# Expert weights in slabs of 1 MB in eighteen places instead of 2 MB in nine

## The chip, the cores and the metric

The kernel runs on one core of a Trainium2 chip. The metric is the time of one launch on the device in microseconds (us); lower is better. All arithmetic is float32. The engines are named as the profile names them: PE (TensorE, the matmuls; PEld its weight loads), DVE (VectorE), ACT (ScalarE), POOL (GpSimd) and SP (SyncE, which here only issues DMAs).

## The reference

One step of a two-layer backbone for 128 context tokens and 256 latent tokens of width 1024. Each layer has three token mixers, a merge, and then a mixture of 16 experts. The change touches only how the weights of the experts reach the core:

```python
def _expert_choice_ffn(h, w_router, w_gate, w_up, w_down):
    cap = EC_FACTOR * n // N_EXPERTS
    aff = jax.nn.softmax(jnp.einsum('bnd,de->bne', h, w_router), axis=-1)
    g, idx = lax.top_k(jnp.swapaxes(aff, 1, 2), cap)
    xg = jax.vmap(lambda hb, ib: hb[ib])(h, idx)
    hid = jax.nn.silu(jnp.einsum('becd,edf->becf', xg, w_gate)) * jnp.einsum('becd,edf->becf', xg, w_up)
    out = jnp.einsum('becf,efd->becd', hid, w_down) * g[..., None]
    ... # added back to the tokens it was taken from
```

Each of `w_gate`, `w_up` and `w_down` is 1024 x 1024 float32 per expert, 4 MB. So 16 experts with three matrices are 192 MB per layer (201.3 million bytes), and nothing of them is used twice.

## The kernel before

The loop over the two layers is a loop on the chip (`nc.Fori`); its body is one block in which each engine has its own program. The programs meet at semaphores: `gate_h`, `up_h`, `down_full` count the slabs of each kind that PE has used, and `expert_in[b]` says that a load into buffer b has landed. In time a layer has a dense part (modulation, the three mixers, projections), the routing (affinities, the choice of tokens), and the expert stage.

The expert stage: an expert's matrix is cut along its rows into two slabs of four row chunks (128 partitions x 4 x 1024, 2 MB, `EXPERT_SLABS = 6` per expert). The slabs go round nine places in SBUF (`EXPERT_BUFFERS = 9`): four are the ring of the dense part, three lie in `dense`, two in `wide`. `EXPERT_ORDER` fixes the order both for SP and for PE: gate and up of expert e + 1 come before down of expert e. SP issues one DMA per slab (`load_expert`); before load i it waits until PE has used slab i - 9 (`wait_used`). PE (`product`) waits at each slab for its landing, runs eight pairs of matmuls (a pair fills two halves of the array, 64 columns each) and then counts the slab as used.

The first three loads are issued between dense slabs 27, 28 and 29, as soon as their places are free (`EARLY`, `buffer_free`); the other six follow as the ring and the two last places come free, all before the expert stage begins. At the end of a layer SP loads the first four modulation slabs of the next layer into the ring (`mod_again`), each after the last expert slab in its place has been used. The one in ring place 0 waits for slab 95, the very last. When all engines are through, `clear_all` sets all the semaphores of the layer to zero, each engine a fifth of them, between two barriers, and the loop jumps back.

The weights are laid out in HBM by `expert_slabs` so that each slab is one contiguous piece, with 16 KB in a row for each partition. The dense part's slabs are fetched in two DMAs of 1 MB each (lines 580 and 581), with 8 KB in a row for each partition.

Of the kernel before, what the change touches and what calls it, by code (L numbers as in the profile page):

```python
# [13 lines left out]
P = 128  # L14
D = 1024
KD = D // P
# [24 lines left out]
DENSE_SLABS = 32  # L41
EXPERT_SLABS = 6
EXPERT_BUFFERS = 9
MOD_AHEAD = 4
# [69 lines left out]
def build(nc, x_in, cvec, cache_kT, cache_v, state_in_dram, w_mod, layer_vectors, layer_scalars,  # L114
# [13 lines left out]
    with ctx:  # L128
# [83 lines left out]
        def ring_slab(r):  # L212
            return slab_shape(ring[:, r].rearrange("p k n -> p (k n)"))
# [5 lines left out]
        wide_1 = slab_shape(wide_cols[:, 4096:8192])  # L219
        BUFFERS = [dense_1, dense_2, wide_1, ring_slab(1), dense_0, ring_slab(0), ring_slab(2), ring_slab(3), wide_0]  # L220
        RING_AT = [5, 3, 6, 7]
# [238 lines left out]
        with nc.Fori(0, DEPTH) as layer:  # L460
            with nc.Block() as block:
# [23 lines left out]
                def mod_parts(j):  # L485
# [9 lines left out]

                EXPERT_ORDER = ([(0, s) for s in range(4)]
                                + [x for e in range(NE) for x in [(e + 1, s) for s in range(4) if e + 1 < NE] + [(e, 4), (e, 5)]])
                assert len(EXPERT_ORDER) == NE * EXPERT_SLABS
# [44 lines left out]
                def _(sp):  # L543
# [4 lines left out]
                    def load_expert(i):  # L548
                        e, s = EXPERT_ORDER[i]
                        w = (w_gate, w_up, w_down)[s // 2]  # L550
                        sp.dma_start(BUFFERS[i % EXPERT_BUFFERS], w[layer, e, s % 2]).then_inc(expert_in[i % EXPERT_BUFFERS], 16)

                    def wait_used(i):
                        e, s = EXPERT_ORDER[i]
                        sp.wait_ge((gate_h, up_h, down_full)[s // 2], 2 * e + s % 2 + 1)

                    EARLY = 3

                    def buffer_free(i):

                        if i < EARLY:
                            sp.wait_ge(c_done, HEADS_C)
                            sp.wait_ge(ko_st, 32)
                            sp.wait_ge(v_stored, 32)
                        elif i == 4:
                            sp.wait_ge(br_full, 3 * KD)
                        elif i == 8:
                            sp.wait_ge(w_full, KD)
                            sp.wait_ge(stored, 32)
                        else:  # L570
                            wait_slab_free(sp, DENSE_SLABS - RING + RING_AT.index(i))

                    for n in range(MOD_AHEAD, DENSE_SLABS):
                        if 27 <= n < 27 + EARLY:
                            buffer_free(n - 27)
                            load_expert(n - 27)
                        wait_slab_free(sp, n - RING)
# [12 lines left out]
                    def mod_again(j):  # L590
                        i = max(i for i in range(NE * EXPERT_SLABS) if i % EXPERT_BUFFERS == RING_AT[j])
                        wait_used(i)
                        mod_ahead(sp, DEPTH - 1 - layer, j)
# [33 lines left out]
                def _(pe):  # L627
# [330 lines left out]
                    def product(expert, s0, bank, signal, lhsT):  # L958

                        for s in (s0, s0 + 1):  # L960
                            i = EXPERT_ORDER.index((expert, s))
                            w = BUFFERS[i % EXPERT_BUFFERS]
                            pe.wait_ge(expert_in[i % EXPERT_BUFFERS], 16 * (i // EXPERT_BUFFERS + 1))
                            for kk in range(KD // 2):
                                k = (s % 2) * (KD // 2) + kk
                                for half in range(2):
                                    last = M.matmul(psum[HALF * half:HALF * (half + 1), bank, :], lhsT(k),  # L967
                                                    w[:, kk, half * SLAB:(half + 1) * SLAB], start=k == 0, stop=k == KD - 1)
                            last.then_inc(signal, 1)
# [15 lines left out]
                    def up_product(expert):  # L985
                        if expert >= 1:
                            pe.wait_ge(hid_ready, expert)
                        product(expert, 2, S[1], up_h, gathered_chunk(expert))

# [8 lines left out]
                    def down_product(expert):  # L998
                        pe.wait_ge(ht_read, expert + 1)
                        if expert >= 1:  # L1000
                            pe.wait_ge(down_act, expert)
                            pe.wait_ge(down_dve, expert)
                        product(expert, 4, TR[1], down_full, lambda k: hidT[:, k % 4, k // 4, :])

# [43 lines left out]
                def _(sc):  # L1048
# [208 lines left out]
                    def silu(expert):  # L1257
                        sc.wait_ge(gate_h, 2 * expert + 2)
                        if expert >= 1:
# [5 lines left out]
                    for e in range(NE):  # L1265
# [5 lines left out]
                        if nth == 2 and quad + 1 < QUADS:  # L1271
                            read_gathered(quad + 1)
                        sc.wait_ge(down_full, 2 * e + 2)
                        for half in range(2):
# [6 lines left out]
                def _(dve):  # L1281
# [269 lines left out]
                    def gated(expert):  # L1551
                        dve.wait_ge(silu_ready, expert + 1)
                        dve.wait_ge(up_h, 2 * expert + 2)
                        if expert >= 1:
# [14 lines left out]
                    for e in range(NE):  # L1569
# [10 lines left out]
                        if nth == 2 and quad + 1 < QUADS:  # L1580
                            read_gathered(quad + 1)
                        dve.wait_ge(down_full, 2 * e + 2)
                        for half in range(2):
# [115 lines left out]
```

## Time and profile before

| | |
|---|---|
| time, median of 3 runs | 2063.16 us (2059.74 to 2064.07) |
| time of the profiled execution | 2063.99 us |
| its span, first to last instruction | 2062.1 us |
| mean granted TensorE clock | 0.984 |
| PE busy | 1857.9 us, 90% of the span |
| read from HBM | 555.30 MB, 271 GB/s over the span |
| expert products of layer 1 on PE | 579.1 to 1018.0 us |
| expert products of layer 2 on PE | to 2034.9 us |

The span is 1.9 us shorter than the execution. The page cuts the span into 40 slices of 51.6 us; a digit is a busy share in tenths. A matmul's float32 operands make two instructions of it, so eight pairs of matmuls are 32 instructions in two slabs and 16 in one. MB in the profile are millions of bytes where it speaks of traffic, and KB are 1024 bytes where it speaks of one DMA: a slab of 2048 KB is 2.097 million bytes.

### The profile page before, as it was taken

To read this page: it belongs to the slowest core of one execution; us is meant where nothing else is said; L and a number is where in the kernel's file an instruction comes from. 1 tells how busy PE (TensorE), PEld (TensorE's weight loads), DVE (VectorE), ACT (ScalarE), POOL (GpSimd) and SP (SyncE) were. 2 spreads that over 40 slices of the span, in tenths; PEclk is the share of its full clock that TensorE was granted. 3 is DMA by queue.
4 is the path that set the end of the run, shared out by engine and by line. 5 is a ranking of instruction groups with operands and counts; after the bars stand their busy time and mean duration, and the time that the engine had idled before them with its cause. 6 is when DMAs were issued, how large, how long until landed. Compare 5 with 4: busy or idle time off the path is not lost. (4 is left out here: it accounts for less than half of the span.)

```text
span 2062.1 us, 20148 instructions
## 1 busy us (share of the span) xinstructions
PE 1857.9 (90%) x8062; PEld 929.3 (45%) x8062; DVE 614.7 (30%) x1179; ACT 336.0 (16%) x771; POOL 36.7 (2%) x22
## 2 busy tenths in 40 slices
PE   5999999999799988788689999999997998888885
PEld 2565556555444333233245555565554343333322
DVE  2332346554311101001142324654534002010103
ACT  4022331000201000000131223210002010100001
POOL 0100000000000000000020000000000000000000
PEclk9999999999999999999989999999998999999998
DMA  9322281433469999999972222816332999999998
GB/s 391 139 92 87 82 349 70 168 158 129 157 284 427 428 427 428 428 427 427 402 307 92 82 87 87 332 41 244 119 142 107 400 427 428 427 427 428 428 427 345
DMA packets 53412, 560.88 MB, mean 272 GB/s; under 512 B 6080, under 2 KB 10816, under 8 KB 12224
## 3 DMA queue, kind: packets, MB, share of 16 engines
q1 hardware_dynamic: 49536, 556.90, 65.2%
q10 hardware_dynamic: 3776, 2.62, 0.4%
q8 instruction: 66, 1.08, 0.2%
q14 instruction: 34, 0.28, 0.0%
HBM read 555.30 MB, written 4.19 MB: 271 GB/s over the span
## 5 line engine op out<-in xcount | busy, mean ns | idle before, releaser
L685 PE MATMUL psum<-hT,ring 128*128 128x384 f32 x768 | 259.5, 493 | 4.1 <-DMA ring<-in_w_in 2.2
L812 PE MATMUL psum<-hT,ring 128*128 128x384 f32 x768 | 255.9, 486 | 1.1 <-issue 1.1
L967 PE MATMUL psum<-dense 128*64 128x512 f32 x864 | 195.4, 596 | 33.4 <-DMA dense<-in_w_up 17.6
L967 PE MATMUL psum<-ring,dense 128*64 128x512 f32 x832 | 188.3, 596 | 25.4 <-DMA ring<-in_w_gate 14.6
L812 PEld LDWEIGHTS psum<-hT,ring 128*128 128x128 f32 x768 | 145.6, 190 | 102.5 <-issue 1.5
L685 PEld LDWEIGHTS psum<-hT,ring 128*128 128x128 f32 x768 | 145.0, 192 | 99.2 <-issue 6.7
L1556 DVE TENSOR_TENSOR state<-state,psum 128x512 f32<-128x512 f32 x32 | 22.0, 688 | 375.3 <-PE psum L967 337.2
L967 PEld LDWEIGHTS psum<-dense 128*64 128x64 f32 x864 | 63.9, 137 | 155.0 <-issue 130.7
L967 PE MATMUL psum<-ring,bwd_decay 128*64 128x512 f32 x512 | 115.3, 596 | 20.1 <-DMA ring<-in_w_down 20.1
L896 PE MATMUL psum<-dense,ring 128*128 128x384 f32 x384 | 131.9, 487 | 0.0
L687 PE MATMUL psum<-ring,hT 128*128 128x512 f32 x288 | 126.5, 592 | 0.0
L1452 DVE RECIPROCAL kcT<-kcT 128x384 f32<-128x384 f32 x48 | 122.6, 2553 | 1.7
L967 PEld LDWEIGHTS psum<-ring,dense 128*64 128x64 f32 x832 | 60.7, 137 | 138.3 <-issue 117.9
L1275 ACT ACTIVATE kcT<-psum 32x512 f32<-32x512 f32 x64 | 37.6, 588 | 480.5 <-PE psum L967 480.1
L896 PEld LDWEIGHTS psum<-dense,ring 128*128 128x128 f32 x384 | 72.8, 190 | 50.6
L1584 DVE COPY q_decay<-psum 16x512 f32<-16x512 f32 x32 | 21.9, 684 | 239.4 <-PE psum L967 239.4
L967 PE MATMUL psum<-wide,dense 128*64 128x512 f32 x352 | 80.1, 597 | 14.0 <-DMA wide<-in_w_gate 13.8
L908 PE MATMUL psum<-wide,ring 128*128 128x384 f32 x256 | 82.9, 486 | 0.0
L687 PEld LDWEIGHTS psum<-ring,hT 128*128 128x128 f32 x288 | 54.3, 190 | 62.2 <-issue 60.3
L967 PE MATMUL psum<-wide,bwd_decay 128*64 128x512 f32 x320 | 72.7, 595 | 10.7 <-DMA wide<-in_w_down 10.7
L660 PE MATMUL psum<-ring,silu_c 128*32 128x512 f32 x384 | 50.1, 649 | 35.5 <-DMA ring<-in_w_mod 21.0
L967 PEld LDWEIGHTS psum<-ring,bwd_decay 128*64 128x64 f32 x512 | 35.8, 137 | 96.9 <-issue 68.6
(201 smaller groups left out, 1579.5 us busy)
## 6 DMA issues: line engine op xcount, KB each, us to landing
ring<-in_w_up SPq DMA_DIRECT2D x32, 2048.0 KB, 38.4
ring<-in_w_down SPq DMA_DIRECT2D x32, 2048.0 KB, 40.2
ring<-in_w_in SPq DMA_DIRECT2D x60, 1024.0 KB, 9.1
dense<-in_w_up SPq DMA_DIRECT2D x30, 2048.0 KB, 40.2
dense<-in_w_gate SPq DMA_DIRECT2D x24, 2048.0 KB, 35.6
ring<-in_w_gate SPq DMA_DIRECT2D x20, 2048.0 KB, 36.8
wide<-in_w_down SPq DMA_DIRECT2D x20, 2048.0 KB, 40.3
wide<-in_w_gate SPq DMA_DIRECT2D x20, 2048.0 KB, 38.3
```

What stands on the lines that cost most here:

```text
L660: last = M.matmul(psum[32 * q:32 * q + 32, bank, :], silu_c[:, k, :], ring[:, n % RING, k, :], start=half == 0, stop=half == 1)
L685: last = M.matmul(psum[:, bank, 0:T], ring[:, n % RING, k, cols], hT[:, k, :], start=k == 0, stop=k == KD - 1)
L687: last = M.matmul(psum[:, bank, :], hT[:, k, cols], ring[:, n % RING, k, :], start=k == 0, stop=k == KD - 1)
L812: last = M.matmul(psum[:, Z[1], 0:T], ring[:, n_gate % RING, k, (j % 4) * P:(j % 4 + 1) * P], hT[:, k, :], start=k == 0, stop=k == KD - 1)
L896: last = M.matmul(psum[:, Z[0], 0:T], w[:, k, j * P:(j + 1) * P], zT[:, source + k, :], start=k == 0, stop=k == 3)
L908: last = M.matmul(psum[:, S[j % 2], 0:T], ring[:, (30 + j // 4) % RING, k, (j % 4) * P:(j % 4 + 1) * P], merged[:, k, :], start=k == 0, st ...
L967: last = M.matmul(psum[HALF * half:HALF * (half + 1), bank, :], lhsT(k), w[:, kk, half * SLAB:(half + 1) * SLAB], start=k == 0, stop=k == ...
L1275: last = A_.activation(out_lat[half][SLOTS * nth:SLOTS * (nth + 1)], psum[HALF * half:HALF * half + CAP_LAT, TR[1], :], ACT.Copy)
L1452: then(V.reciprocal(g, g))
L1556: V.tensor_tensor(hid, act, psum[:, S[1], :], ALU.mult).then_inc(hid_ready, 1)
L1584: last = V.tensor_copy(out_ctx[half][SLOTS * nth:SLOTS * nth + CAP_CTX], psum[HALF * half + CAP_LAT:HALF * half + ROWS, TR[1], :])
```

## The change

A matrix is cut into four slabs of two row chunks (1 MB), each of the nine places is halved into two buffers, and every count goes over from 2 to `PER_PRODUCT = 4` slabs per matrix. The layout in HBM changes with it: a slab is again one contiguous piece, now with 8 KB in a row for each partition. The places, the order of the matrices, the matmuls and the bytes are the same; the first three places are still filled early, now with two loads each. Nine semaphores are added.

```diff
@@ -39,8 +39,9 @@
 SLAB = 512
 RING = 4
 DENSE_SLABS = 32
-EXPERT_SLABS = 6
-EXPERT_BUFFERS = 9
+EXPERT_SLABS = 12
+PER_PRODUCT = 4
+EXPERT_BUFFERS = 18
 MOD_AHEAD = 4
 
 DVE_MODULATES = ((0, 2, 3, 5, 6), (2, 4, 7))
@@ -217,7 +218,8 @@
         dense_2 = slab_shape(dense[:, DENSE - 4096:DENSE])
         wide_0 = slab_shape(wide_cols[:, 0:4096])
         wide_1 = slab_shape(wide_cols[:, 4096:8192])
-        BUFFERS = [dense_1, dense_2, wide_1, ring_slab(1), dense_0, ring_slab(0), ring_slab(2), ring_slab(3), wide_0]
+        PLACES = [dense_1, dense_2, wide_1, ring_slab(1), dense_0, ring_slab(0), ring_slab(2), ring_slab(3), wide_0]
+        BUFFERS = [place[:, 2 * half:2 * half + 2, :] for place in PLACES for half in range(2)]
         RING_AT = [5, 3, 6, 7]
         assert len(BUFFERS) == EXPERT_BUFFERS
 
@@ -493,8 +495,8 @@
                             + [(6, j, "T") for j in range(4)] + [(7, j, "rows") for j in range(NBLK)]
                             + [(8, j, "T") for j in range(4)])
 
-                EXPERT_ORDER = ([(0, s) for s in range(4)]
-                                + [x for e in range(NE) for x in [(e + 1, s) for s in range(4) if e + 1 < NE] + [(e, 4), (e, 5)]])
+                EXPERT_ORDER = ([(0, s) for s in range(8)]
+                                + [x for e in range(NE) for x in [(e + 1, s) for s in range(8) if e + 1 < NE] + [(e, s) for s in range(8, 12)]])
                 assert len(EXPERT_ORDER) == NE * EXPERT_SLABS
                 UNITS = 12
                 A_STEPS = UNITS + 2
@@ -547,18 +549,19 @@
                     sp.dma_start(kcT[:], cache_kT[layer]).then_inc(keys_in, 16)
                     def load_expert(i):
                         e, s = EXPERT_ORDER[i]
-                        w = (w_gate, w_up, w_down)[s // 2]
-                        sp.dma_start(BUFFERS[i % EXPERT_BUFFERS], w[layer, e, s % 2]).then_inc(expert_in[i % EXPERT_BUFFERS], 16)
+                        w = (w_gate, w_up, w_down)[s // PER_PRODUCT]
+                        sp.dma_start(BUFFERS[i % EXPERT_BUFFERS], w[layer, e, s % PER_PRODUCT]).then_inc(expert_in[i % EXPERT_BUFFERS], 16)
 
                     def wait_used(i):
                         e, s = EXPERT_ORDER[i]
-                        sp.wait_ge((gate_h, up_h, down_full)[s // 2], 2 * e + s % 2 + 1)
-
-                    EARLY = 3
+                        sp.wait_ge((gate_h, up_h, down_full)[s // PER_PRODUCT], PER_PRODUCT * e + s % PER_PRODUCT + 1)
+
+                    EARLY = 6
 
                     def buffer_free(i):
 
-                        if i < EARLY:
+                        i = i // 2
+                        if i < 3:
                             sp.wait_ge(c_done, HEADS_C)
                             sp.wait_ge(ko_st, 32)
                             sp.wait_ge(v_stored, 32)
@@ -571,9 +574,10 @@
                             wait_slab_free(sp, DENSE_SLABS - RING + RING_AT.index(i))
 
                     for n in range(MOD_AHEAD, DENSE_SLABS):
-                        if 27 <= n < 27 + EARLY:
-                            buffer_free(n - 27)
-                            load_expert(n - 27)
+                        if 27 <= n < 30:
+                            for i in (2 * (n - 27), 2 * (n - 27) + 1):
+                                buffer_free(i)
+                                load_expert(i)
                         wait_slab_free(sp, n - RING)
                         to, of = slab_into(n), slab_source(n)
                         half = to.shape[1] // 2
@@ -588,7 +592,7 @@
                                 sp.dma_start(bias[b], rpb_bias[layer, b]).then_inc(bias_in, 16)
 
                     def mod_again(j):
-                        i = max(i for i in range(NE * EXPERT_SLABS) if i % EXPERT_BUFFERS == RING_AT[j])
+                        i = max(i for i in range(NE * EXPERT_SLABS) if i % EXPERT_BUFFERS == 2 * RING_AT[j] + 1)
                         wait_used(i)
                         mod_ahead(sp, DEPTH - 1 - layer, j)
 
@@ -957,12 +961,12 @@
 
                     def product(expert, s0, bank, signal, lhsT):
 
-                        for s in (s0, s0 + 1):
+                        for s in range(s0, s0 + PER_PRODUCT):
                             i = EXPERT_ORDER.index((expert, s))
                             w = BUFFERS[i % EXPERT_BUFFERS]
                             pe.wait_ge(expert_in[i % EXPERT_BUFFERS], 16 * (i // EXPERT_BUFFERS + 1))
-                            for kk in range(KD // 2):
-                                k = (s % 2) * (KD // 2) + kk
+                            for kk in range(2):
+                                k = (s % PER_PRODUCT) * 2 + kk
                                 for half in range(2):
                                     last = M.matmul(psum[HALF * half:HALF * (half + 1), bank, :], lhsT(k),
                                                     w[:, kk, half * SLAB:(half + 1) * SLAB], start=k == 0, stop=k == KD - 1)
@@ -985,7 +989,7 @@
                     def up_product(expert):
                         if expert >= 1:
                             pe.wait_ge(hid_ready, expert)
-                        product(expert, 2, S[1], up_h, gathered_chunk(expert))
+                        product(expert, PER_PRODUCT, S[1], up_h, gathered_chunk(expert))
 
                     def hidden_transposed(expert):
                         pe.wait_ge(hid_ready, expert + 1)
@@ -1000,7 +1004,7 @@
                         if expert >= 1:
                             pe.wait_ge(down_act, expert)
                             pe.wait_ge(down_dve, expert)
-                        product(expert, 4, TR[1], down_full, lambda k: hidT[:, k % 4, k // 4, :])
+                        product(expert, 2 * PER_PRODUCT, TR[1], down_full, lambda k: hidT[:, k % 4, k // 4, :])
 
                     def picks_transposed(quad):
                         pe.wait_ge(pick_g_ready, quad + 1)
@@ -1255,7 +1259,7 @@
                                           psum[:, XG[part], :].rearrange("p (k s) -> p k s", s=CAP_LAT), ACT.Copy).then_inc(xg_act, 1)
 
                     def silu(expert):
-                        sc.wait_ge(gate_h, 2 * expert + 2)
+                        sc.wait_ge(gate_h, PER_PRODUCT * (expert + 1))
                         if expert >= 1:
                             sc.wait_ge(hid_ready, expert)
                         A_.activation(act, psum[:, S[0], :], ACT.Silu).then_inc(silu_ready, 1)
@@ -1270,7 +1274,7 @@
                         A_.activation(hidT.rearrange("p q h s -> p (q h s)"), psum[:, TR[0], :], ACT.Copy).then_inc(ht_read, 1)
                         if nth == 2 and quad + 1 < QUADS:
                             read_gathered(quad + 1)
-                        sc.wait_ge(down_full, 2 * e + 2)
+                        sc.wait_ge(down_full, PER_PRODUCT * (e + 1))
                         for half in range(2):
                             last = A_.activation(out_lat[half][SLOTS * nth:SLOTS * (nth + 1)], psum[HALF * half:HALF * half + CAP_LAT, TR[1], :], ACT.Copy)
                         last.then_inc(down_act, 1)
@@ -1550,7 +1554,7 @@
 
                     def gated(expert):
                         dve.wait_ge(silu_ready, expert + 1)
-                        dve.wait_ge(up_h, 2 * expert + 2)
+                        dve.wait_ge(up_h, PER_PRODUCT * (expert + 1))
                         if expert >= 1:
                             dve.wait_ge(ht_full, expert)
                         V.tensor_tensor(hid, act, psum[:, S[1], :], ALU.mult).then_inc(hid_ready, 1)
@@ -1579,7 +1583,7 @@
                             gated(e + 1)
                         if nth == 2 and quad + 1 < QUADS:
                             read_gathered(quad + 1)
-                        dve.wait_ge(down_full, 2 * e + 2)
+                        dve.wait_ge(down_full, PER_PRODUCT * (e + 1))
                         for half in range(2):
                             last = V.tensor_copy(out_ctx[half][SLOTS * nth:SLOTS * nth + CAP_CTX], psum[HALF * half + CAP_LAT:HALF * half + ROWS, TR[1], :])
                         last.then_inc(down_dve, 1)
@@ -1658,7 +1662,7 @@
         return w.reshape(d, rows // P, P, n, cols // n).transpose(0, 3, 2, 1, 4)
 
     def expert_slabs(w):
-        return w.reshape(DEPTH, NE, 2, KD // 2, P, D).transpose(0, 1, 2, 4, 3, 5)
+        return w.reshape(DEPTH, NE, 4, 2, P, D).transpose(0, 1, 2, 4, 3, 5)
 
     feeds = [
         ("x", x.reshape(T, KD, P).transpose(2, 1, 0)),
```

On SP, around the start of the expert stage: before, with the last loads into fresh places and the first refills. The names `gate_h` and `up_h` are the counts of gate and up slabs used by PE.

```order
L551 DMA ring<-in_w_up 128x4096 [waits w_full] x2
L551 DMA wide<-in_w_down 128x4096 [waits stored,w_full]
L551 DMA dense<-in_w_down 128x4096 [waits gate_h]
L551 ISA [waits gate_h]
L551 DMA dense<-in_w_gate 128x4096
```

The same place after the change:

```order
L553 DMA ring<-in_w_up 128x2048 [waits w_full] x4
L553 DMA wide<-in_w_down 128x2048 [waits stored,w_full] x2
L553 DMA dense<-in_w_down 128x2048 [waits gate_h] x2
L553 ISA [waits gate_h]
L553 DMA dense<-in_w_gate 128x2048
L553 ISA [waits gate_h]
L553 DMA dense<-in_w_gate 128x2048
```

Each load has become two of half the width, with a wait of its own before each; nothing has changed places.

On PE, the last products of a layer (down of expert 15) and what follows them, before:

```order
L967 MATMUL psum<-dense,bwd_decay 64x512 [waits down_dve,expert_in4,down_act,ht_read]
L967 MATMUL psum<-dense,bwd_decay 64x512 x7
L967 MATMUL psum<-ring,bwd_decay 64x512 [waits expert_in5]
L967 MATMUL psum<-ring,bwd_decay 64x512 x7
L1024 MATMUL psum<-square,q_decay 128x128 [waits pgT_read,down_dve,down_act]
```

And after:

```order
L971 MATMUL psum<-dense,bwd_decay 64x512 [waits down_dve,expert_in8,down_act,ht_read]
L971 MATMUL psum<-dense,bwd_decay 64x512 x3
L971 MATMUL psum<-dense,bwd_decay 64x512 [waits expert_in9]
L971 MATMUL psum<-dense,bwd_decay 64x512 x3
L971 MATMUL psum<-ring,bwd_decay 64x512 [waits expert_in10]
L971 MATMUL psum<-ring,bwd_decay 64x512 x3
L971 MATMUL psum<-ring,bwd_decay 64x512 [waits expert_in11]
L971 MATMUL psum<-ring,bwd_decay 64x512 x3
L1028 MATMUL psum<-square,q_decay 128x128 [waits pgT_read,down_dve,down_act]
```

Behind the wait for the last load there stand 4 matmuls of this listing where there were 8.

The semaphores cleared by PE at the end of a layer, before and after:

```order
L397 ISA x26
```

```order
L399 ISA x27
```

PE has one more; SP has 28 instead of 26, and the other three engines have 27 instead of 25.

## Rows read from the trace of the kernel before

**Rows 1.** The page, slices of 51.6 us: DMA share in tenths and rate.
```profile
DMA  9322281433469999999972222816332999999998
GB/s 391 139 92 87 82 349 70 168 158 129 157 284 427 428 427 428 428 427 427 402 307 92 82 87 87 332 41 244 119 142 107 400 427 428 427 427 428 428 427 345
```
**Rows 2.** Windows: length, busy of each engine, PEclk, DMA share, GB/s.
```profile
560.00:580.00 20.00, 11.40 (x82) 10.37 (x82) 9.42 (x34) 5.76 (x10) 0.00 (x0) 0.83 0.00 1
600.00:1000.00 400.00, 349.61 (x1690) 136.27 (x1691) 52.97 (x104) 37.62 (x64) 0.00 (x0) 1.00 1.01 428
1620.00:2010.00 390.00, 342.12 (x1658) 133.90 (x1654) 52.28 (x103) 36.47 (x62) 0.00 (x0) 1.00 1.01 428
```
**Rows 3.** The page's DMA issues: count, KB each, median us to landing.
```profile
ring<-in_w_up SPq DMA_DIRECT2D x32, 2048.0 KB, 38.4
ring<-in_w_down SPq DMA_DIRECT2D x32, 2048.0 KB, 40.2
```
**Rows 4.** Timeline of PE: stage start, then end of layer 1.
```profile
579.10 7.09 PE L967 MATMUL psum<-dense 128*64 128x512 f32 x32 [0.83 <-issue]
585.99 3.63 PE L967 MATMUL psum<-wide,dense 128*64 128x512 f32 x16
...
999.77 3.65 PE L967 MATMUL psum<-wide,bwd_decay 128*64 128x512 f32 x16 [1.33 <-DMA wide<-in_w_down]
1004.59 3.65 PE L967 MATMUL psum<-ring,bwd_decay 128*64 128x512 f32 x16 [1.16 <-DMA ring<-in_w_down]
1008.17 0.66 PE L429 MATMUL psum<-const,state 128*128 128x128 f32 x4
1010.15 3.65 PE L967 MATMUL psum<-dense,bwd_decay 128*64 128x512 f32 x16 [1.32 <-ACT bwd_decay L1270]
1014.37 3.65 PE L967 MATMUL psum<-ring,bwd_decay 128*64 128x512 f32 x16 [0.57 <-DMA ring<-in_w_down]
1019.57 0.46 PE L1024 MATMUL psum<-square,q_decay 128*128 128x128 f32 x2 [1.55 <-ACT kcT L1275]
```
**Rows 5.** Timeline of SP's DMA issues: stage start, then end of layer 1.
```profile
547.56 0.33 SPq L551 DMA_DIRECT2D wide<-in_w_down  x1
582.78 0.33 SPq L551 DMA_DIRECT2D dense<-in_w_down  x1
586.35 0.33 SPq L551 DMA_DIRECT2D dense<-in_w_gate  x1
...
1008.53 11.07 SPq L416 DMA_DIRECT2D ring<-in_w_mod  x4
```
**Rows 6.** Windows of 20 us in which loads of 8 KB rows fill the queue.
```profile
275.00:295.00 20.00, 16.59 (x148) 8.08 (x150) 7.78 (x21) 7.08 (x22) 0.00 (x0) 1.00 1.01 424
1293.00:1313.00 20.00, 17.09 (x156) 7.97 (x157) 7.72 (x21) 7.18 (x21) 0.00 (x0) 1.00 1.01 424
272.00:292.00 20.00, 17.41 (x156) 8.58 (x158) 8.81 (x25) 7.17 (x22) 0.00 (x0) 1.00 1.00 418
1290.00:1310.00 20.00, 17.40 (x158) 8.40 (x150) 7.79 (x21) 6.99 (x21) 0.00 (x0) 1.00 1.01 419
```
**Rows 7.** Timeline of PE: the first matmul of layer 2.
```profile
1036.21 4.50 PE L660 MATMUL psum<-ring,silu_c 128*32 128x512 f32 x20 [11.16 <-issue]
```
**Rows 8.** PE's semaphore clears by their line: ns min/median/max.
```profile
L397 PEldq EVENT_SEMAPHORE_RANGE_CLEAR  x53: 56/56/63, 10.5 to 2046.1; - x53
```
**Rows 9.** Timeline of SP: the slowest issues of loads in layer 2.
```profile
1049.62 1.01 SPq L580 DMA_DIRECT2D ring<-in_w_in  x1
1050.81 1.97 SPq L581 DMA_DIRECT2D ring<-in_w_in  x1
```

## The prediction

> **What bounds the kernel now.** I read the slices first. In both layers there is a stretch of eight slices, the expert stage, in which the DMA digit is 9 and the rate stands at 427 or 428 GB/s [rows 1]. Over 400 us of it in layer 1 and 390 us in layer 2 the mean is 428 GB/s and the 16 DMA engines are fully busy, while PE is busy for 349.61 of 400 us [rows 2]. So the transfers set the pace there. The second look is at the landing times: a 2 MB load lands 38.4 to 40.2 us after its issue [rows 3]. One slab takes 2,097,152 bytes / 428 GB/s = 4.90 us, so about eight loads are queued all the time. PE takes a slab as it lands (1.15 to 1.33 us of waiting before slabs that it then works through in some 3.4 us [rows 4]) and gives its place back at once.
>
> The third look is at both ends of this stream. Before the stage all nine places are full and the DMA engines stand still: the last load into a fresh place is issued at 547.56, and the rate is 1 GB/s from 560 to 580 [rows 2, 5]. PE starts the first product at 579.10; 32 instructions, two slabs, take until 585.99, so one slab takes 3.44 us [rows 4]. The first refill is issued at 582.78 [rows 5], which is 579.10 + 3.44 + 0.24. From there 96 - 9 = 87 slabs have to come: 87 x 4.90 = 426.3 us, and with 5.3 us for the start and the landing that makes the 431.6 us until the last one is there at 1014.37 [rows 4]. PE then needs 3.65 us for the whole last slab before the results can be read and scattered. Layer 2 has the same shape. So three things of this stage are on the path to the end: when the first place comes free, the rate, and how much work is left once the last bytes are in.
>
> **The change part by part.**
>
> The start. The first place comes free after half a slab, 3.44 / 2 = 1.72 us earlier. The first refill has only 1 MB, 2.45 us of transfer, but the next is issued 1.72 us later, so the stream doesn't stop, just as now 3.57 us lie between issues and 4.90 us are needed [rows 5]. The whole stream moves forward: -1.72 us in each layer. The bounds are 0, if the start of the stream costs more with small loads, and the whole 1.72.
>
> The end. After the last landing there stand 4 pairs of matmuls instead of 8: 3.65 / 2 = 1.83 us, of which I take 1.72 by the pace of the start. What else could be late then? The slab before it started at 1010.15, held up by the transposed hidden values and not by its data: these came after down of expert 14, whose last slab landed at 1004.59 [rows 4]. That step also shrinks by half a slab, so it is ready by about 1008.4, and PE has 1014.37 - 1008.4 = 6.0 us for the three quarter-matrices before the last, 5.2 us of work. It is just through when the last 1 MB lands. Then -1.72 us in each layer; the bound on the other side is 0 if the last megabyte has to queue behind something.
>
> The two ends together: 4 x 1.72 = 6.9 us to gain.
>
> The rate. The trace has no 1 MB expert load, but the dense part loads its slabs in halves of 1 MB with 8 KB rows, and twice several of them stand in the queue together. In the stretches 275 to 295 and 1293 to 1313 the DMA engines are as busy as in the expert stage and move 424 GB/s. Windows that begin 3 us earlier show 418 and 419 [rows 6]; the queue is just filling up in these, so I take 424. Then the stream of a layer takes 426.3 x (428/424 - 1) = 4.0 us longer, 8.0 us in both. Bounds: 0 (nothing is lost by the smaller rows: the windows are short, and 1% of 20 us is 0.2 us, less than one packet of each engine), and 426.3 x (428/418 - 1) = 10.2 us in each layer. The nearest rows are the full windows, so the value is 4.0.
>
> The Trainium skill, "DMA: Bandwidth & Descriptors", section "Measured (HBM→SBUF, 128 partitions, SWDGE, issued from GpSimd)", warns against small transfers: a fixed 2.0 us per DMA beside the bytes at 436 GB/s. If each queued load paid that, a layer's 87 slabs of 2 MB would take 87 x 6.8 = 592 us by an estimate from that page, and 174 halves 766; the trace disagrees, with 431.6 us, because eight loads are queued and the fixed part lies beside them. Its section "Why small descriptors are slow (HBM only)" gives about 3 cycles per packet on top of one per 32 bytes. As an estimate from that, two rows of 8 KB cost 2 x 259 cycles against 515, 0.58% more, 2.5 us per layer in place of 4.0; the sum below would then be -1.7 us instead of +1.3. The direction agrees with 424 against 428, and the size can't be told from windows of 20 us.
>
> SP. It issues 174 refills per layer instead of 87. An issue takes 0.33 us [rows 5], against 2.45 us of transfer, so it keeps up, and what stands behind it in its queue is only the next load. With twice as many loads outstanding the issue itself may stall, as it does when many dense loads are queued (1.01 and 1.97 us [rows 9]); that is still under 2.45 us, and the queue is full when it happens. Cost 0. PE has a wait per 4 pairs instead of 8; where the data are there, two slabs follow each other without a gap [rows 4], so 0 as well.
>
> The end of the layer. The next layer's first matmul comes 11.16 us after the last of this one [rows 7]; in that gap the semaphores are cleared. One more clear on PE is 0.056 us [rows 8], with what lies around it I take 0.1, per layer; bounds 0 and the whole gap divided by 26, 0.43. Sum 0.2 us. The modulation slabs of the next layer are issued as before after the last expert slab (four issues from 1008.53 on [rows 5]); they shift forward with it. Instructions of PE's program and the matmuls stay as they are.
>
> The sum: -6.9 + 8.0 + 0.2 = +1.3 us on the profiled execution's 2063.99, so 2065.3. The median of the runs shown is 2063.16, 0.8 us below the profiled one; measured against it the forecast is 2064.5 us.
>
> **The rivals.** About 0.2% (4.1 us) is what a measurement of this kernel can tell from no change.
>
> Rival 1, the rate isn't touched. For it: the engines are over 100% busy in both kinds of stretches, packets overlap, and the sample of 8 KB rows is 40 us long. Against it: two separate windows show the same 424. It gives -6.9 + 0.2 = -6.7 us, 2057.3 on the profiled execution and 2056.5 against the median: faster. It counts as faster as soon as the rate is at least 427.
>
> Rival 2, the stream of small loads is slower than the best windows. Mechanism: the DMA queue in the expert stage with 1 MB loads, each with its own completion, and PE, which has no slack against it. The mean of the four windows in rows 6 is 421 GB/s. Then the two streams cost 2 x 426.3 x (428/421 - 1) = 14.2 us, and the sum is -6.9 + 14.2 + 0.2 = +7.5 us, 2071.5 or 2070.7 against the median: slower. It decides where the loss is above 6.9 + 4.1 - 0.2 = 10.8 us, which is a rate under 422.6. For it: the windows of 418 and 419. Against: these begin while the queue fills.
>
> Rival 3, SP's issue becomes the bound. If every issue of a 1 MB load took longer than 2.45 us, the stream would be issue-bound; at 2.6 us it would cost 174 x 0.15 = 26 us in each layer. The longest single issue of these loads seen is 1.97 us [rows 9]. Unlikely.
>
> Rival 4, the small slabs don't bring the stream forward, because the rate in its first microseconds or the landing of the last load is set by something else. Then the gain is half or less: -3.4 + 8.0 + 0.2 = +4.8 us, 2068.8. For it: 5.3 us of the 431.6 aren't explained by bytes. Against: the refill is issued when a count of PE moves, and that is plain in rows 4 and 5.
>
> **How the numbers follow.** Forecast 0.50, rival 1 0.26, rival 2 0.16, rival 3 0.02, rival 4 0.06. Faster than before by over 0.2%: 0.26. Within: 0.50. Slower: 0.16 + 0.02 + 0.06 = 0.24. The forecast's own range is 2060.5 to 2067.4, from rates of 426 to 422.6. For 8 in 10 the range takes in rivals 1 and 2: 2056 to 2071.
>
> **What would show it.** In the changed profile: the first refill issued about 1.7 us nearer to the first product than the 3.68 us of now; the last landing followed by about 1.8 us of products; a window over the stage with 424 GB/s; about sixteen loads queued, so again some 40 us to landing; and the stage from its first product to its last longer by 4.0 - 3.4 = 0.6 us than now. A rate of 427 or more would make the forecast wrong on the fast side, one of 421 on the slow side. A DMA share under 1 in the stage would point to SP.

## The result

| | before | after |
|---|---|---|
| median of 11 runs each | 2063.16 us | 2072.93 us |
| ratio, 95% interval | 1 | 1.0038 (1.0029 to 1.0046) |
| profiled execution | 2063.99 us | 2071.03 us |
| span | 2062.1 us | 2068.9 us |

The change makes the kernel slower: 0.38%, 7.8 us (6.0 to 9.5). The two medians alone lie further apart, 9.8 us; the means of the 11 runs are 2064.0 and 2072.0 us. The profiled executions differ by 7.0 us, the spans by 6.8.

The windows of the kernel after come first (length, busy of each engine, PEclk, DMA share, GB/s), against [rows 2] and [rows 6]: the expert stages of both layers, then the four stretches of the dense part.

```profile
600.00:1000.00 400.00, 357.77 (x1684) 129.05 (x1686) 52.27 (x103) 37.61 (x64) 0.00 (x0) 1.00 1.01 421
1620.00:2010.00 390.00, 349.29 (x1648) 126.56 (x1648) 52.29 (x103) 36.46 (x62) 0.00 (x0) 1.00 1.01 421
...
275.00:295.00 20.00, 16.63 (x149) 8.14 (x151) 7.78 (x21) 7.23 (x22) 0.00 (x0) 1.00 1.01 424
1293.00:1313.00 20.00, 17.41 (x156) 8.19 (x149) 7.98 (x22) 6.82 (x22) 0.00 (x0) 1.00 1.01 419
272.00:292.00 20.00, 17.42 (x160) 8.61 (x160) 8.89 (x25) 7.32 (x23) 0.00 (x0) 1.00 1.00 417
1290.00:1310.00 20.00, 17.12 (x152) 8.91 (x152) 9.44 (x28) 8.15 (x26) 0.00 (x0) 1.00 0.99 408
```

The DMA engines are as full as before, and the rate of the expert stage is 421 GB/s instead of 428. The dense part was not changed. Its windows of layer 1 read 424 and 417, and 424 and 418 before [rows 6]. Those of layer 2 read 419 and 408 instead of 424 and 419, but by then this kernel is 3.25 us later in its work (the first matmul of layer 2 starts at 1039.46 instead of 1036.21 [rows 7]). Moved by these 3.25 us, the two windows read 424 and 419, as before:

```profile
1296.25:1316.25 20.00, 17.18 (x158) 7.99 (x157) 7.70 (x21) 7.28 (x21) 0.00 (x0) 1.00 1.01 424
1293.25:1313.25 20.00, 17.41 (x158) 8.39 (x150) 7.78 (x21) 7.00 (x21) 0.00 (x0) 1.00 1.01 419
```

So the 424 of the dense part comes back in another execution, and it still isn't the rate of the expert stage with 1 MB loads. Nor is a single window of 20 us exact: the 20 windows of that length between 600 and 1000 us read 424 to 429 GB/s before and 419 to 422 after.

The timeline of SP after, the last fill and the first refills:

```profile
548.15 1.07 SPq L553 DMA_DIRECT2D wide<-in_w_down  x2
581.09 2.05 SPq L553 DMA_DIRECT2D dense<-in_w_down  x2
584.65 2.05 SPq L553 DMA_DIRECT2D dense<-in_w_gate  x2
```

PE's timeline after, from the first product, and the end of layer 1:

```profile
579.12 7.09 PE L971 MATMUL psum<-dense 128*64 128x512 f32 x32 [0.83 <-issue]
...
1009.13 1.94 PE L971 MATMUL psum<-ring,bwd_decay 128*64 128x512 f32 x8 [0.56 <-DMA ring<-in_w_down]
1011.00 0.66 PE L431 MATMUL psum<-const,state 128*128 128x128 f32 x4
1012.98 3.65 PE L971 MATMUL psum<-dense,bwd_decay 128*64 128x512 f32 x16 [1.32 <-ACT bwd_decay L1274]
1016.58 1.94 PE L971 MATMUL psum<-ring,bwd_decay 128*64 128x512 f32 x8
1019.06 1.94 PE L971 MATMUL psum<-ring,bwd_decay 128*64 128x512 f32 x8 [0.54 <-DMA ring<-in_w_down]
1022.54 0.46 PE L1028 MATMUL psum<-square,q_decay 128*128 128x128 f32 x2 [1.55 <-ACT kcT L1279]
...
1039.46 6.55 PE L664 MATMUL psum<-ring,silu_c 128*32 128x512 f32 x32 [11.44 <-issue]
```

The first refill goes out 581.09 - 579.12 = 1.97 us after the first product instead of 3.68 [rows 4, 5]. The scatter begins 1022.54 - 1019.06 = 3.48 us after the last landing instead of 5.20 [rows 4]. Both ends gave the 1.7 us that was expected of them. But the last landing is 1019.06 - 579.12 = 439.94 us after the first product, where it was 435.27. From the first product to the scatter (the matmuls that add the experts' results back to the tokens), which I call the stage, it is 443.42 us, and was 1019.57 - 579.10 = 440.47. That is +2.95 us in layer 1. In layer 2 it is 2042.90 - 1599.27 = 443.63 against 440.41, +3.22 us. The gap with the semaphore clears is 0.28 us longer [rows 7].

The page's DMA issues after, answering to [rows 3]:

```profile
ring<-in_w_up SPq DMA_DIRECT2D x64, 1024.0 KB, 26.9
ring<-in_w_down SPq DMA_DIRECT2D x64, 1024.0 KB, 26.8
```

And SP's issues by the load's line, durations in ns, min/median/max:

```profile
L553 SPq DMA_DIRECT2D ring<-in_w_up x64: 332/2070/7792, 503.3 to 1957.7; - x64
```

A load lands after 26.9 us, not after some 40, and an issue takes 2.07 us instead of 0.33: SP stands at the issue. At 2.49 us per load 10.8 loads are on their way, not sixteen. That the issue waits for room in the queue is a reading; the run with a short queue below bears it out.

### The profile page after: what moved, and what is told of

Read it like the earlier page. It is cut to its first block and busy times, and to the rows that moved or that the text cites. A ratio compares the mean times of both kernels' runs of the same rounds, so it can differ in the third digit from the quotient of the medians.

```text
span 2068.9 us, 20622 instructions
## 1 busy us (share of the span) xinstructions
PE 1877.9 (91%) x8062; PEld 914.7 (44%) x8062; DVE 613.4 (30%) x1179; ACT 335.7 (16%) x771; POOL 36.4 (2%) x22
## 5 line engine op out<-in xcount | busy, mean ns | idle before, releaser
L971 PE MATMUL psum<-dense 128*64 128x512 f32 x864 | 201.5, 599 | 28.3 <-DMA dense<-in_w_up 15.4
L971 PE MATMUL psum<-ring,dense 128*64 128x512 f32 x832 | 194.0, 599 | 21.6 <-DMA ring<-in_w_gate 13.1
L971 PE MATMUL psum<-ring,bwd_decay 128*64 128x512 f32 x512 | 119.6, 600 | 18.5 <-DMA ring<-in_w_down 18.5
L971 PEld LDWEIGHTS psum<-dense 128*64 128x64 f32 x864 | 59.1, 136 | 160.3 <-issue 105.1
L971 PEld LDWEIGHTS psum<-ring,dense 128*64 128x64 f32 x832 | 56.2, 136 | 144.4 <-issue 95.3
L664 PE MATMUL psum<-ring,silu_c 128*32 128x512 f32 x384 | 49.9, 646 | 36.3 <-DMA ring<-in_w_mod 21.6
## 6 DMA issues: line engine op xcount, KB each, us to landing
ring<-in_w_up SPq DMA_DIRECT2D x64, 1024.0 KB, 26.9
wide<-in_w_down SPq DMA_DIRECT2D x40, 1024.0 KB, 26.9
```

The source lines that it names most:

```text
L664: last = M.matmul(psum[32 * q:32 * q + 32, bank, :], silu_c[:, k, :], ring[:, n % RING, k, :], start=half == 0, stop=half == 1)
```

## The experiments

What has to be explained is the rate. Theory A: rows of 8 KB cost more than rows of 16 KB. Theory B: the number of DMAs, each with a completion. Theory C: the stalled issues, or the full queue. Unless another is named, each comparison is with the kernel before, which was run again beside each group of experiments (medians 2064.81, 2064.97 and 2063.94 us); a difference in us is worked out from the ratio.

**Rows of 8 KB in 2 MB loads (e_rows8).** Nine places and 2 MB per DMA as before; only the layout and the two views of it change:

```diff
-  sp.dma_start(BUFFERS[i % EXPERT_BUFFERS], w[layer, e, s % 2]).then_inc(...)
+  sp.dma_start(BUFFERS[i % EXPERT_BUFFERS].rearrange("p (h k) n -> p h (k n)", h=2),
+               w[layer, e, s % 2].rearrange("h p k n -> p h (k n)")).then_inc(...)
-  return w.reshape(DEPTH, NE, 2, KD // 2, P, D).transpose(0, 1, 2, 4, 3, 5)
+  return w.reshape(DEPTH, NE, 2, 2, 2, P, D).transpose(0, 1, 2, 3, 5, 4, 6)
```

> The kernel before, still with 2 MB loads in nine places and one completion per 2 MB, but the weights laid out so that each load has 256 rows of 8 KB instead of 128 rows of 16 KB. The change's rate of 421 GB/s against 428 (4.98 against 4.90 us per 2 MB) is to be explained. Theory A, the rows: each row costs its engine something fixed; then this kernel streams at 421 to 422 too, loses 6.8 us in each layer, has neither of the two gains, and takes about 13.6 us longer than before, 2077 us. Theory B, the number of DMAs (each with its own completion): then it stays at 428 and at 2063 us. In the change the loads were issued with stalls and landed after 26.9 us instead of 40.2; if what is limited is the number of rows and completions queued on an engine (10.8 loads x 9 = 97 in the change), here 5 to 6 loads are queued and they land after some 28 us; if it is the number of DMAs, they land after 40.

Measured: 1.0065 (1.0050 to 1.0081), 13.4 us. The windows over the stages:

```profile
600.00:1000.00 400.00, 346.23 (x1672) 134.84 (x1670) 52.29 (x103) 37.50 (x64) 0.00 (x0) 1.00 1.01 421
1620.00:2010.00 390.00, 339.88 (x1645) 132.92 (x1643) 51.32 (x102) 35.29 (x60) 0.00 (x0) 1.00 1.01 421
```

The page's DMA issues:

```profile
ring<-in_w_up SPq DMA_DIRECT2D x32, 2048.0 KB, 32.5
```

PE's timeline, first product, last slab and scatter of layer 1:

```profile
579.00 7.09 PE L967 MATMUL psum<-dense 128*64 128x512 f32 x32 [0.83 <-issue]
...
1020.64 3.65 PE L967 MATMUL psum<-ring,bwd_decay 128*64 128x512 f32 x16 [0.74 <-DMA ring<-in_w_down]
1025.84 0.46 PE L1024 MATMUL psum<-square,q_decay 128*128 128x128 f32 x2 [1.55 <-ACT kcT L1275]
```

The row length alone makes 421 out of 428, with the number of loads and completions unchanged. The stage takes 1025.84 - 579.00 = 446.84 us, 6.4 us more than before, and 447.20 in layer 2, 6.8 more. The sum is 13.2, as the runs say. Theory B isn't needed. On the queue I was halfway off: loads land after 32.5 us, which is 6.5 loads of 16 rows and a completion per engine, 111 of them, against 97 in the change. So it is not the number of DMAs that is limited, and not exactly this count either; what sets the length of the queue stays open.

**Two DMAs of 64 partitions each (e_parts64).** The counterpart, rows of 16 KB in 1 MB loads:

```diff
+  for part in (slice(0, HALF), slice(HALF, P)):
+      sp.dma_start(BUFFERS[i % EXPERT_BUFFERS][part], w[layer, e, s % 2][part]).then_inc(...)
```

PE waits for a count of 32 instead of 16 per slab.

> The kernel before, each 2 MB slab fetched by two DMAs of 1 MB with 64 partitions each, so the rows stay at 16 KB and only the number of DMAs and completions doubles. Theory A (rows): 428 GB/s, 2063 us. Theory B (number of DMAs): 421 GB/s, some 13.6 us longer, 2077 us. A third possibility is that half the partitions at a time don't spread evenly over the ports and the rate falls by much more; then it says nothing of either.

Measured: 1.4079 (1.4050 to 1.4108), 2906.5 us; the third possibility. The window over the stage:

```profile
600.00:1000.00 400.00, 247.01 (x880) 86.10 (x878) 25.02 (x46) 19.99 (x34) 0.00 (x0) 0.81 1.01 214
```

The DMA engines are shown as busy, and move half. It says nothing of A or B. Why is not in this trace. The Trainium skill, "DMA: Bandwidth & Descriptors", section "The descriptor swizzle", has 128 partitions spread over sixteen SBUF ports with the lower 64 on eight of them, which would fit, and which no run here shows.

**Two DMAs of two row chunks each (e_two_dmas).** The change's transfers with the coarse grain of before:

```diff
+  for c in (slice(0, 2), slice(2, 4)):
+      sp.dma_start(BUFFERS[i % EXPERT_BUFFERS][:, c], w[layer, e, s % 2][:, c]).then_inc(...)
```

> The kernel before with its nine places and its grain of use, but each 2 MB slab fetched by two DMAs of 1 MB with 8 KB rows, as the change does. Both theories of the rate expect 421 GB/s here. It has the change's transfers without its earlier refill and shorter end, so it should be the change plus 6.9 us: 2080 us or 1.0081 of before, against 1.0038 for the change. If it equals the change, the two ends bring nothing.

Measured: 1.0061 (1.0046 to 1.0075), 12.6 us. Its windows:

```profile
600.00:1000.00 400.00, 346.62 (x1676) 134.97 (x1674) 52.29 (x103) 37.62 (x64) 0.00 (x0) 1.00 1.01 421
1620.00:2010.00 390.00, 338.78 (x1640) 132.21 (x1638) 52.28 (x103) 36.46 (x62) 0.00 (x0) 1.00 1.01 421
```

With twice the DMAs of e_rows8 it has the same rate and within the intervals the same time: the number of DMAs costs nothing here. Theory B falls. The two kernels also read HBM differently, e_rows8 from slabs laid out anew for it, e_two_dmas half of each 16 KB row of the old layout. As both run at 421 GB/s, the layout in HBM isn't the cause either. Its stages take 446.86 and 446.78 us, the change's 443.42 and 443.63, so the finer grain is worth 3.44 and 3.15 us per layer in the profiles; by the ratios it is 4.7 us in all, with intervals that take in 6.6.

**Rows of 4 KB (e_rows4).** As e_rows8, with four pieces of one row chunk per load (`h=4`, and a reshape to `2, 4, 1` in place of `2, 2, 2`).

> The kernel before with 2 MB loads in nine places, but each load has 512 rows of 4 KB. If each row costs its engine a fixed time, the cost must go on in proportion: 8 KB rows made 4.90 us per 2 MB (428 GB/s) into 4.98 (421) with 8 more rows per engine, so 24 more rows make 5.14 us, 408 GB/s, 87 x 0.24 = 21 us in each layer and 42 us in all, 1.020 of before. If the loss came from the layout in HBM or from the queue of the issues and not from the rows, there is no reason for three times the loss.

Measured: 1.0176 (1.0160 to 1.0191), 36.3 us (33 to 39.4); stages 459.59 and 459.62 us, 38.3 us more in both together. The expected 42 was too much, though the rate is near:

```profile
600.00:1000.00 400.00, 337.56 (x1632) 131.78 (x1630) 52.28 (x103) 36.47 (x62) 0.00 (x0) 1.00 1.03 409
1620.00:2010.00 390.00, 333.99 (x1617) 131.53 (x1615) 50.34 (x100) 34.71 (x59) 0.00 (x0) 1.00 1.02 408
```

At 428, 421 and 409 GB/s 2 MB take 4.90, 4.98 and 5.13 us with 8, 16 and 32 rows on each engine. That is 10.2 ns for each of the first 8 additional rows and 9.5 ns as the mean over 24. As the rates are whole GB/s, the first figure is good to about 1.5 ns: the cost goes with the number of rows.

**The change with a short queue (e_short_queue).**

```diff
-                            wait_used(i - EXPERT_BUFFERS)
+                            wait_used(i - (EXPERT_BUFFERS if i < 72 else 9))
```

> The change, but from load 72 of 192 on a load waits for the use of the slab nine before it instead of eighteen, so that at most nine 1 MB loads are queued. In the change SP stood at its issues (2.1 us each) and the loads landed after 26.9 us; here the issues should take 0.33 us again and the loads land after some 22 us. Theory A (rows): the rate stays at 421 and the time at that of the change, 1.0038 of before. Theory C (the stalled issue or the full queue costs the rate): the rate goes back to 428 from load 72 on, the time falls by some 9 us and comes out below before, 0.9995 or less.

Measured: 1.0044 (1.0029 to 1.0059), the change's own time within the intervals. SP's issues by the load's line:

```profile
L553 SPq DMA_DIRECT2D ring<-in_w_up x64: 332/333/6245, 503.3 to 1967.3; - x64
```

The window behind load 72:

```profile
800.00:1000.00 200.00, 171.18 (x788) 59.68 (x785) 27.26 (x57) 17.67 (x30) 0.00 (x0) 1.00 1.01 421
```

The median issue is back at 0.333 us, loads land after 20.3 us (8.2 of them on their way), and the rate stays at 421. Its stages take 444.10 and 444.50 us, 0.7 and 0.9 more than the change's, so nothing is gained without the stalls. Theory C falls. A queue shorter than eight loads wasn't tried.

**The ends without the loss.** If rows are the cause, a kernel with 16 KB rows that halves only a few loads should have both gains. First with three halved loads (e_hybrid; `LAST` is 93 and 95 of the 96 slabs):

```diff
+  if i == EXPERT_BUFFERS:
+      sp.wait_ge(half_used, 1)      # PE counts it after half of slab 0
+      sp.dma_start(at[:, 0:2], of[:, 0:2]).then_inc(landed, 16)
+      wait_used(0)
+      sp.dma_start(at[:, 2:4], of[:, 2:4]).then_inc(landed, 16)
+  elif i in LAST:
+      sp.dma_start(at[:, 0:2], of[:, 0:2]).then_inc(landed, 16)
+      sp.dma_start(at[:, 2:4], of[:, 2:4]).then_inc(last_in[LAST.index(i)], 16)
+  else:
...
```

> The kernel before with 2 MB loads and 16 KB rows, but three loads of a layer halved: the first refill (its first half goes out when PE has used half of slab 0) and slabs 93 and 95 of 96, whose halves PE takes one at a time. Both theories of the rate expect 428 GB/s in the stage, and both gains of the change without its loss: 1.72 us at the start and 1.72 us at the end of each layer, 6.9 us in all less 0.2 for four more semaphores, so 2056.5 us or 0.9968 of before. If the loss of the change lay in anything but the steady stream, it would not reach this.

Measured: 0.9994 (0.9985 to 1.0002). A miss. Its timeline at the end of layer 2:

```profile
2017.18 3.65 PE L983 MATMUL psum<-wide,bwd_decay 128*64 128x512 f32 x16 [1.34 <-DMA wide<-in_w_down]
2020.64 3.63 PE L983 MATMUL psum<-ring,bwd_decay 128*64 128x512 f32 x16
2024.20 0.66 PE L433 MATMUL psum<-const,state 128*128 128x128 f32 x4
2027.06 3.65 PE L983 MATMUL psum<-dense,bwd_decay 128*64 128x512 f32 x16 [2.20 <-DMA dense<-in_w_down]
2030.51 3.63 PE L983 MATMUL psum<-ring,bwd_decay 128*64 128x512 f32 x16
2035.68 0.46 PE L1042 MATMUL psum<-square,q_decay 128*128 128x128 f32 x2 [1.54 <-ACT kcT L1293]
```

Slab 94, which I had left whole, is waited for (2.20 us), and two whole slabs of work stand behind its landing. In layer 1 the wait is nearly the same, and there the slab also takes 5.34 us instead of 3.65, at a lower granted clock (last section):

```profile
1011.90 5.34 PE L983 MATMUL psum<-dense,bwd_decay 128*64 128x512 f32 x16 [2.16 <-DMA dense<-in_w_down]
```

The stages take 440.02 and 439.11 us. Slab 94 split too (e_hybrid3, `LAST` is 93, 94 and 95):

> The earlier kernel with three halved loads, now also with slab 94 halved (four in all). There the profile showed the end of the layer held up by slab 94: it landed whole, and PE had 3.44 + 3.44 us of work after it. With all of the last three slabs in halves the last landing should be followed by 1.8 us of products. From the first product to the scatter a layer should take 440.5 - 3.4 = 437.0 us (before: 440.5 and 440.4), and the kernel 0.9967 of before. If it comes out at 0.998 or above, something else takes back what the ends give.

Measured: 0.9991 (0.9981 to 1.0002), a miss again. Its first product, last half slab and scatter in layer 1:

```profile
584.88 7.09 PE L983 MATMUL psum<-dense 128*64 128x512 f32 x32 [0.83 <-issue]
...
1021.56 1.94 PE L983 MATMUL psum<-ring,bwd_decay 128*64 128x512 f32 x8 [0.42 <-DMA ring<-in_w_down]
1025.04 0.46 PE L1042 MATMUL psum<-square,q_decay 128*128 128x128 f32 x2 [1.54 <-ACT kcT L1293]
```

The end is right, 3.48 us. But the last landing comes 436.68 us after the first product, later than the 435.27 of before, though the first refill was early and the rate is 428. So the two halves of the idea were tried apart. Only the last three loads halved (e_end):

> The kernel before with only the last three loads of a layer halved (93, 94 and 95 of 96), nothing else. In the kernel with four halved loads the last landing was followed by 3.48 us to the scatter instead of 5.20, but it came 1.4 us later after the first product than before, so a stage took 440.1 us instead of 440.5. If the early first refill is what disturbed the stream, then here the last landing is where it was before (435.3 us after the first product), the stage takes 438.7 us and the kernel 0.9983 of before. If the halved last loads are themselves late, the stage takes 440 us again and the kernel 0.999 to 1.000.

Measured: 0.9984 (0.9976 to 0.9993), 3.3 us faster than before. It is the lowest ratio of this study and the only one whose whole interval lies below 1. First product, last half and scatter:

```profile
580.85 7.09 PE L977 MATMUL psum<-dense 128*64 128x512 f32 x32 [0.83 <-issue]
...
1016.20 1.94 PE L977 MATMUL psum<-ring,bwd_decay 128*64 128x512 f32 x8 [0.44 <-DMA ring<-in_w_down]
1019.68 0.46 PE L1034 MATMUL psum<-square,q_decay 128*128 128x128 f32 x2 [1.54 <-ACT kcT L1285]
```

The last landing is at 435.35 us, the stage takes 438.83, and 438.84 in layer 2, as expected. Only the first refill halved (e_start):

> The kernel before with only the first refill of a layer halved, its first half issued 1.7 us earlier; the last loads are whole. If that brings the stream forward as it does in the change (last landing 1.7 us earlier than with the same rate and late refill), the stage takes 440.5 - 1.7 = 438.8 us and the kernel 0.9983 of before. If it disturbs the stream, as the kernel with four halved loads suggests, the last landing comes no earlier than before and the kernel is at 1.000 or above.

Measured: 0.9999 (0.9989 to 1.0008). In its profile the last whole slab lands 1014.57 - 580.20 = 434.37 us after the first product, 0.9 us earlier than before, and the stages take 439.57 and 439.24 us. So it brought 0.9 and 1.2 us instead of 1.7 in the profile, and nothing that the runs can tell. The bytes moved, read from the traces in layer 1, say where a part goes. In its first 10 us from the first product the change moves 2.70 MB, 0.77 MB more than e_rows8 (1.93); that is 1.8 us of transfer. e_start moves 2.54 MB, 0.52 MB more than the kernel before (2.02), and it keeps this lead: after 400 us it is still 0.49 MB, or 1.1 us. So what is missing was lost at once, in the first 10 us of the stage. In e_hybrid3 the lead is 0.50 MB after 10 us and 0.36 MB after 400, and yet its last slab lands 1.4 us later than before; the bytes don't say to which load they belong, nor which of the 16 engines lands last. Why the early halves of e_start and e_hybrid3 bring less than those of the change stays open.

## Why the prediction was wrong

The forecast was 2064.5 us and no change, the range ended at 2071.0; the median is 2072.93, and 1.0038 times the old median is 2071.0. So the result lies at or beyond the upper end, and the forecast of no change did not come true.

- What bounds the kernel: right. The DMA stream sets the pace, and every difference of rate shows in the time. (Of the eight slices that it calls 427 or 428 in each layer, seven are; the last reads 402, in layer 2 the first reads 400 [rows 1]. Nothing hangs on that.)
- "The start", -1.72 us per layer: right. With the same rate and whole slabs (e_rows8) the last landing is at 1020.64 - 579.00 = 441.64 us, in the change at 439.94, 1.70 earlier.
- "The end", -1.72: right, 5.20 to 3.48 us. A slab is four pairs of matmuls and not eight, so two pairs stand behind the last landing where four stood; it is half either way.
- "The rate", 4.0 us per layer: this step failed, by its size. The mechanism was there, smaller rows at a full queue. But I took the 424 GB/s of the dense part for the rate of the expert stage, and that was 421. The term is 6.4 us in layer 1 and 6.8 in layer 2 (e_rows8 against before), 13.2 us in place of 8.0. That is 5.2 of the 6.5 us between +1.3 and the 7.8 measured.
- The reading of the windows themselves holds. The 424 came back in the profile after, and the 418 and 419 do take in the filling of the queue: in the kernel before, 270 to 275 us moves 356 GB/s and 1288 to 1293 us 382. Inside the full window of layer 1 the first 10 us read 426 and the last 10 us 423 (425 and 422 after), so 424 wasn't a steady rate. Why the dense part still reads more than 421 is open. Its loads land 13.2 to 15.1 us after their issue in that window, so five or six are on their way, fewer than in any experiment with 1 MB loads.
- Rival 2 forecast +7.5 us, nearly what was measured, but by luck: its 421 is the mean of two full windows and of two that begin in the filling. With 0.16 it was given too little all the same, since a window of 20 us can be off by 4 GB/s even in the steady stage, and 3 GB/s are 3 us in each layer.
- The estimate from the Trainium skill's three cycles per packet ("DMA: Bandwidth & Descriptors", "Why small descriptors are slow (HBM only)"), 0.58%, is too small as well: 428 to 421 is 1.6%.
- The fixed 2 us per DMA of the same page, set aside there: right to do so, e_two_dmas doubles the DMAs at the same rate. The figure stands in that page's section "Anatomy of one DMA — SWDGE (gpsimd) path", for DMAs issued from GpSimd, and not in the section that the prediction names; the loads here are issued from SP.
- "SP", cost 0: right in the price, wrong in the picture. I expected sixteen queued loads and 40 us to landing; SP stands at its issues instead and 10.8 loads are on their way, at no cost (e_short_queue).
- The clears, +0.1 per layer: the gap grew by 0.28 us in layer 1 and by 0.11 in layer 2. Not all of the 0.28 need be clears: in e_rows8, which has the semaphores of before, the same gap is 11.32 us, 0.16 longer.
- Rival 4 (the start brings little or nothing) did not happen in the change, but in e_start it did in part.

With the terms as the profiles have them the sum is -7.0 (the change's stages against those of e_rows8, 3.42 and 3.57 us) + 13.2 + 0.4 (the gaps) = +6.6 us; the spans differ by 6.8. The rest, up to the 7.8 us of the runs, is inside their interval.

## What to carry to other kernels

Where the DMA queue is always full, as in this stage, the length of the contiguous row for each partition is a price on every byte (428, 421 and 409 GB/s here); a finer grain pays only once at each end of the stream. So keep the long rows in the stream and halve only the last loads, all of those that PE still has before it when the last bytes land: that gave 0.9984 where halving everything gave 1.0038. And a rate read in one part of a kernel is no more than an estimate for another part. Where 3 GB/s decide between two forecasts, give the term the spread that windows of that length show in a steady stretch.

## What was not expected of the hardware

Each additional row cost an engine about 10 ns, in steps from 16 to 8 to 4 KB (428, 421, 409 GB/s). Loads of 64 partitions, the lower and the upper half in turn, ran at 214 GB/s, half of the rate, with all DMA engines shown as busy.

TensorE's granted clock in the routing before the stage differs between the profiled executions of kernels whose work there is the same. Windows of e_hybrid, in the routing and in its slab 94:

```profile
555.00:560.00 5.00, 4.37 (x16) 1.10 (x16) 4.00 (x11) 3.51 (x9) 0.00 (x0) 0.50 0.95 406
570.00:575.00 5.00, 2.05 (x10) 1.98 (x11) 3.23 (x10) 0.00 (x0) 0.00 (x0) 0.50 0.00 0
1010.00:1015.00 5.00, 3.10 (x8) 1.18 (x10) 0.59 (x1) 0.97 (x2) 0.00 (x0) 0.69 1.01 424
```

The same windows before:

```profile
555.00:560.00 5.00, 3.86 (x24) 1.58 (x22) 3.11 (x10) 1.93 (x5) 0.00 (x0) 0.76 0.73 315
570.00:575.00 5.00, 4.02 (x22) 3.94 (x22) 1.32 (x3) 0.22 (x1) 0.00 (x0) 0.55 0.00 0
1010.00:1015.00 5.00, 4.28 (x20) 1.40 (x22) 0.00 (x0) 0.10 (x1) 0.00 (x0) 1.00 1.01 423
```

A value of 0.50 is the level of 1.2 GHz, the lower of the two. The first product stood at 579.10 us before, at 582.20 in e_hybrid and at 584.88 in e_hybrid3. The wait before slab 94 doesn't decide it alone: in e_hybrid PE had stood for 2.16 us before it in layer 1, where the slab took 5.34 us, and for 2.20 us in layer 2, where it took 3.65.

The kernel before varies in the same way by itself. Over the 55 executions of it that stand beside the experiments, those with a mean clock of 0.984 took 2062.4 to 2065.8 us and those with 0.982 took 2066.5 to 2069.0. Such shifts are of the size of the effects here; that is why the stages are compared from their own first product.
